# A two-layer transformer chain on one core: Strassen products in all three feed-forward up stages, with half of the weight sums made by adding DMAs

## The chip, the cores and the metric

One core of one Trainium2 chip runs the whole program. The metric is the device time in microseconds of one execution. Three executions were timed; one more was profiled.

## The reference, cut to what matters

The block works on 528 tokens (16 meta tokens and 512 of the sequence) of width 1024. It has forgetting attention, an HGRN2 mixer and a hybrid mixer (retention and stick-breaking attention), each followed by a feed-forward. The change concerns the three feed-forwards. Stages 0 and 1 are the convolutional ones of the first block, stage 2 is the plain one of the second block and works on 512 tokens.

```python
D_FF = ((8 * D_MODEL // 3 + 127) // 128) * 128

def conv_ffn(h, norm_g, w_gate, w_up, conv_w, conv_b, w_down):
    xn = rms_norm(h, norm_g)
    a = xn @ w_gate
    L = a.shape[1]
    a_pad = jnp.pad(a, ((0, 0), (CONV_WIDTH - 1, 0), (0, 0)))
    a = (conv_b + conv_w[0] * a_pad[:, 0:L] + conv_w[1] * a_pad[:, 1:L + 1]
         + conv_w[2] * a_pad[:, 2:L + 2])
    return (jax.nn.silu(a) * (xn @ w_up)) @ w_down
```

All inputs are float32, and the result has to keep about that precision.

## The kernel before

**Layout.** Activations are kept with features on the partitions: `h` is 128 x 8 x 528 (`KT` = 8 feature tiles, `L` = 528 tokens, `META` = 16, `FT` = 22 hidden tiles). A float32 product is made of three passes on TensorE. Every operand is split into a rounded high part and a remainder (`xh`, `xl` for activations, `wh`, `wl` for weights), and the passes are `wh*xh`, `wh*xl` and `wl*xh`. ScalarE rounds a weight unit into `wh` (`act_hi`, L448), VectorE makes the remainder `wl` (`dve_lo`, L452). SyncE (SP) loads weight units of 8 x 128 x 128 (512 KB) into the four slots of `raw`; `wh` and `wl` have two slots each. A slot of `raw` is loaded again once the unit in it has been split.

**Phases.** A `Phase` is a run of n iterations of groups. A group (`pe_group`, L460 to L494) is one output tile of 128 features: 8 k tiles, three passes, and two halves of 264 columns (L489), or one matmul of 512 columns for a "narrow" group (L485). Its sum lies in a pair of PSUM banks, which VectorE reads. Each engine has its own program; what orders the work is the order in which each engine's instructions are written, and the semaphores between them (`mm_done`, `psum_free`, `w_hi`, `w_split`, `w_loaded0` to `3`, `x_ready`, `hid_ready`).

**The up stages 0 and 1** (`PH_UP0`, `PH_UP1`; `up` on ScalarE from L1378 and on VectorE from L2084) have 11 iterations of four groups: gate tile, up tile, gate tile, up tile. VectorE scales the gate by `rstd` out of PSUM into `pre`, ScalarE and VectorE do the three taps of the convolution (L1391, L2101, L2104), ScalarE the silu, VectorE scales the up tile and multiplies (L2111), and the hidden tile is split into `hidh` (L1327) and `hidl` (L2118) at once. In stage 1 the up groups are narrow. The down stage follows, 8 groups of 22 k tiles, and VectorE adds each to the residual (`residual`, `dve_add_h`), makes `xh` and `xl` for the next stage, and goes on.

**The up stage 2** already uses a Strassen scheme (Winograd's form) for 18 of its 22 hidden tiles: after `PH_UP2` (2 iterations of classic groups) comes `PH_DUO2`. A "pair" there is one gate tile and one up tile. The 8 k tiles are cut into two fours, the 512 tokens into two halves of 256 columns (`h1`, `h2`), so gate and up together are a 2 x 2 by 2 x 2 block product. It takes 7 half products of 4 k tiles x 3 passes (84 matmuls of 256 columns, L1281) in place of 8. The sums of the x halves (`xa`, `xb`, `xc`, `xd`) are made once, by VectorE and ScalarE, during the classic iterations. The four sums of the weights of a pair are made by VectorE (`w_sum`, L2810). The seven weight pieces use four half slots of `wh` and `wl`, so a piece is rounded (ScalarE) and its remainder made (VectorE, `duo_lo`, L2814) only when the piece that had its slot before has been multiplied. The results of the products are combined by ScalarE, which copies two out of PSUM (`p_one` and the first half of `pre`), and VectorE, which makes five combinations from PSUM (L2851, L2855, L2864, L2877, L2828) and scales by `rstd` (L2880). Each hidden tile is kept in float32 (`hid2`), since the x sums lie where the rounded hidden tiles go; most of the splits of the hidden tiles are made at the end of the stage and early in the down stage.

**GpSimd (POOL)** sums squares for the norms, loads tables, and does little else; its DMAs in the attention (`crep`, L1963) are its largest use. In the up stages it has no work.

The functions that the change touches:

Of the kernel before, what the change touches and what calls it, by code (L numbers as in the profile page):

```python
# [15 lines left out]
F32 = mybir.dt.float32  # L16
# [3 lines left out]
ALU = mybir.AluOpType  # L20
# [56 lines left out]

class Phase:
# [26 lines left out]
FOX_STEPS, HG_STEPS = 3 * (FOX_H // 2), 3 * HG_H  # L105
# [9 lines left out]
PH_UP1 = Phase(PH_HGOUT, FT // 2, K8, narrow=(1, 3))  # L115
PH_DOWN1 = Phase(PH_UP1, 2, [list(DOWN_K)] * 4, narrow=range(4))
# [15 lines left out]
PH_UP2 = Phase(PH_OUT, 2, K8, [(1, 3, 2 * (_g % 2), 2 - 2 * (_g % 2))[(b - _g) % 4] for b in range(4)], narrow=range(4))  # L132
PH_DUO2 = Phase(PH_UP2, FT // 2 - PH_UP2.n, K8)
PH_DOWN2 = Phase(PH_DUO2, 2, [list(DOWN_K)] * 4, narrow=range(4))

DUO_SLOT, DUO_BANK = (0, 1, 2, 3, 0, 1, 2), (4, 5, 6, 7, 4, 6, 7)
DUO_RANK, DUO_RANK0 = (2, 3, 4, 1, 5, 6, 7), (1, 2, 3, 4, 5, 6, 7)
DUO_FREE = (-2, -1, 0, -3, 1, 2, 3)  # L140
DUO_PAIRS = 2 * PH_DUO2.n
DUO_W = SEQ // 2
# [43 lines left out]
def program(nc, ctx, dram, out):  # L186
# [118 lines left out]
    hid2 = place("hid2", [P, FT, L], F32, arena + 4 * FT * L)[0]  # L305
    a = Area(arena + 3 * 4 * L, arena + 4 * FT * L)

    def x_sum(name):
        at = a.at
        hi, lo = (a.take(f"{name}{part}", [P, KT // 2, DUO_W], F32R) for part in ("h", "l"))  # L310
        return hi, lo, place(f"{name}f", [P, KT // 2, DUO_W], F32, at + 4 * KT // 2 * DUO_W)[0]

    xb, xc, xa = x_sum("xb"), x_sum("xc"), x_sum("xa")
    w_sum1, w_sum2 = (a.take(n, [P, KT // 2, P]) for n in ("w_sum1", "w_sum2"))
    xd = x_sum("xd")
    x_tmp = place("x_tmp", [P, KT // 2, DUO_W], F32, norms_at + 4 * 5 * L)[0]
    p_one, p_two, p_three = sq[:, 0, 0:DUO_W], sq[:, 0, DUO_W:2 * DUO_W], sq[:, 1, 0:DUO_W]
    h1, h2 = slice(META, META + DUO_W), slice(META + DUO_W, L)
# [198 lines left out]
    def dve_x(dve, rx, m, gain_row, t0=0):  # L517
        dve.wait_ge(s("xh_ready"), KT * rx + 1 + m)
        nc.vector.scalar_tensor_tensor(row(xl, m)[:, t0:L], row(h, m)[:, t0:L], col(gains, m + gain_row),  # L519
                                       row(xh, m)[:, t0:L].bitcast(F32), ALU.mult, ALU.subtract).then_inc(s("x_ready"), 1)  # L520
# [2444 lines left out]
```

## Time and profile before

| | us |
|---|---|
| median of 3 runs | 2821.1 (2818.9 to 2822.27) |
| profiled execution, time | 2822.06 |
| profiled execution, span | 2820.4 |
| granted TensorE clock, mean | 0.993 of full |
| TensorE matmuls busy | 2751.6 (98%) |
| VectorE busy | 1702.2 (60%) |
| ScalarE busy | 1252.3 (44%) |
| GpSimd busy | 186.0 (7%) |

Times in the profile are microseconds unless marked ns. PE is TensorE, PEld its weight loads, DVE VectorE, ACT ScalarE, POOL GpSimd, SP SyncE; an engine's name with a q is its queue or sequencer. Matmuls are pipelined, so one that lasts 285 ns may start 122 ns after the one before; the distance of the starts is what counts. A row of a timeline gives start, duration, engine, line, operation, output and inputs, how many instructions are merged in it, and in brackets the idle time before it and what ended that.

### The profile page before, as it was taken

To read this page: it belongs to the slowest core of one execution; us is meant where nothing else is said; L and a number is where in the kernel's file an instruction comes from. 1 tells how busy PE (TensorE), PEld (TensorE's weight loads), DVE (VectorE), ACT (ScalarE), POOL (GpSimd) and SP (SyncE) were. 2 spreads that over 40 slices of the span, in tenths; PEclk is the share of its full clock that TensorE was granted. 3 is DMA by queue.
4 is the path that set the end of the run, shared out by engine and by line. 5 is a ranking of instruction groups with operands and counts; after the bars stand their busy time and mean duration, and the time that the engine had idled before them with its cause. 6 is when DMAs were issued, how large, how long until landed. Compare 5 with 4: busy or idle time off the path is not lost.

```text
span 2820.4 us, 48705 instructions
## 1 busy us (share of the span) xinstructions
PE 2751.6 (98%) x18309; PEld 2492.4 (88%) x18309; DVE 1702.2 (60%) x2639; ACT 1252.3 (44%) x2071; POOL 186.0 (7%) x160
## 2 busy tenths in 40 slices
PE   7999999999989999999999999999999999899998
PEld 7899899999989999899988887888799988689986
DVE  6777745554367776655543453644577776589932
ACT  4445543332245555433322232232478884455632
POOL 2000010000021221000001010010100000100000
PEclk9999999999999999999999999999999999999999
DMA  4222123332331111233333322323222112223332
GB/s 124 68 75 67 53 81 92 89 89 83 94 98 53 53 55 49 68 97 89 97 89 98 94 68 85 92 70 97 72 71 60 58 58 85 76 83 104 103 90 76
DMA packets 417679, 225.74 MB, mean 80 GB/s; under 512 B 7493, under 2 KB 414278, under 8 KB 417462
## 3 DMA queue, kind: packets, MB, share of 16 engines
q1 hardware_dynamic: 414550, 211.45, 26.2%
q0 software_dynamic: 2256, 10.32, 1.2%
q10 hardware_dynamic: 784, 2.75, 0.3%
q8 instruction: 60, 0.98, 0.1%
q14 instruction: 29, 0.24, 0.0%
HBM read 222.36 MB, written 2.13 MB: 80 GB/s over the span
## 4 chain that ended last, share of the span: by engine, by line
PE 56%; DVE 4%; issue 2%; ACT 1%; POOL 0%; DVEq 0%; POOLq 0%; ACTq 0%
PE ps L485 27%; PE ps L489 14%; PE ps L1281 6%; PE ps L1122 2%; PE ps L1163 1%; PE ps L1152 1%; PE ps L1184 1%; PE ps L964 1%; PE ps L1089 1%; DVE wl L452 1%; PE ps L1075 0%; DVE rl L2554 0%; PE ps L1156 0%; PE ps L1110 0%; PE ps L1103 0%
## 5 line engine op out<-in xcount | busy, mean ns | idle before, releaser
L448 ACT ACTIVATE wh<-raw 128x1024 fp32r<-128x1024 f32 (+3 forms) x386 | 385.7, 1001 | 604.8 <-PE ps L489 335.1
L452 DVE TENSOR_TENSOR wl<-raw,wh 128x1024 fp32r<-128x1024 f32 (+3 forms) x386 | 461.8, 1196 | 316.7 <-ACT wh L448 313.7
L489 PE MATMUL ps<-xh,wh 128*128 128x264 f32 x2736 | 569.8, 289 | 9.8 <-DVE xl L519 5.8
L489 PE MATMUL ps<-xl,wh 128*128 128x264 f32 x2736 | 558.4, 285 | 0.0
L489 PE MATMUL ps<-xh,wl 128*128 128x264 f32 x2736 | 558.3, 286 | 0.0
L489 PEld LDWEIGHTS ps<-xh,wh 128*128 128x128 f32 x2736 | 428.8, 189 | 19.6 <-issue 8.8
L489 PEld LDWEIGHTS ps<-xl,wh 128*128 128x128 f32 x2736 | 425.9, 189 | 0.0
L489 PEld LDWEIGHTS ps<-xh,wl 128*128 128x128 f32 x2736 | 425.2, 189 | 0.0
L485 PE MATMUL ps<-xh,wh 128*128 128x512 f32 x672 | 269.4, 401 | 3.5 <-DVE wl L452 3.5
L485 PE MATMUL ps<-xl,wh 128*128 128x512 f32 x672 | 265.7, 395 | 0.0
L485 PE MATMUL ps<-xh,wl 128*128 128x512 f32 x672 | 264.3, 393 | 0.0
L485 PEld LDWEIGHTS ps<-xh,wh 128*128 128x128 f32 x672 | 126.2, 188 | 34.6 <-issue 6.1
L485 PEld LDWEIGHTS ps<-xh,wl 128*128 128x128 f32 x672 | 126.4, 188 | 28.6
L485 PEld LDWEIGHTS ps<-xl,wh 128*128 128x128 f32 x672 | 126.1, 188 | 28.3 <-issue 1.4
L485 PE MATMUL ps<-hidh,wh 128*128 128x512 f32 x352 | 139.6, 396 | 3.9 <-issue 3.5
L485 PE MATMUL ps<-hidh,wl 128*128 128x512 f32 x352 | 139.5, 396 | 0.0
L485 PE MATMUL ps<-hidl,wh 128*128 128x512 f32 x352 | 138.7, 394 | 0.0
L2063 DVE TENSOR_TENSOR rt<-ps,rstd 128x512 f32<-128x512 f32 (+1 forms) x53 | 37.0, 698 | 140.2 <-PE ps L485 100.7
L2063 DVE TENSOR_TENSOR pre<-ps,rstd 128x528 f32<-128x528 f32 (+1 forms) x48 | 33.9, 706 | 121.8 <-PE ps L489 110.4
L532 POOL COPY ssq<-sq 128x528 f32<-128x528 f32 (+1 forms) x6 | 4.6, 760 | 1345.8 <-ACT sq L515 1075.7
L1978 POOL TENSOR_TENSOR g_d<-post_t 128x528 f32<-128x528 f32 (+1 forms) x56 | 68.5, 1241 | 246.6 <-ACT g_e L1533 158.4
L485 PEld LDWEIGHTS ps<-hidh,wh 128*128 128x128 f32 x352 | 66.5, 189 | 19.2 <-issue 3.7
(444 smaller groups left out, 5177.9 us busy)
## 6 DMA issues: line engine op xcount, KB each, us to landing
raw<-in_w_in SPq DMA_DIRECT2D x88, 512.0 KB, 4.1
raw<-in_ffn_w_gate SPq DMA_DIRECT2D x44, 512.0 KB, 3.8
raw<-in_ffn_w_up SPq DMA_DIRECT2D x44, 512.0 KB, 3.8
raw<-in_w_ffn_in SPq DMA_DIRECT2D x44, 512.0 KB, 4.1
raw<-in_fox_w_in SPq DMA_DIRECT2D x33, 512.0 KB, 4.1
raw<-in_hgrn_w_in SPq DMA_DIRECT2D x32, 512.0 KB, 4.1
raw<-in_ffn_w_down SPq DMA_DIRECT2D x32, 448.0 KB, 3.6
raw<-in_ffn_w_down SPq DMA_DIRECT2D x16, 512.0 KB, 3.8
```

The costliest lines, as they stand in the source:

```text
L448: nc.scalar.activation(wh[:, v % 2, 0:nk, :], raw[:, v % RAW_SLOTS, 0:nk, :], ACT.Copy).then_inc(s("w_hi"), 1)
L452: nc.vector.tensor_tensor(wl[:, v % 2, 0:nk, :], raw[:, v % RAW_SLOTS, 0:nk, :], wh[:, v % 2, 0:nk, :].bitcast(F32), ALU.subtract).then_in ...
L485: last = nc.tensor.matmul(ps[:, bank, 0:SEQ], w[:, slot, kk, :], x[:, k0 + k, x.shape[2] - SEQ:x.shape[2]], start=first, stop=end_)
L489: last = nc.tensor.matmul(ps[:, bank + b, 0:HALF], w[:, slot, kk, :], x[:, k0 + k, b * HALF:(b + 1) * HALF], start=first, stop=end_)
L964: last = nc.tensor.matmul(ps[:, 2 + k % 2, P * c:P * (c + 1)], left[:, P * c:P * (c + 1)], right[:, P * c:P * (c + 1)], start=True, stop=True)
L1089: last = nc.tensor.matmul(flat[0:TOK[j], at:at + SEQ - QFIRST[j]], rt[:, 2 + c, P * j:P * j + TOK[j]], rt[:, c, META + QFIRST[j]:L], start ...
L1122: last = nc.tensor.matmul(ps[:, 4 + e, QFIRST[j]:SEQ], r_vt[0:k, j, P * e:P * (e + 1)], r_s[0:k, QSTRIP[j]:QSTRIP[j] + SEQ - QFIRST[j]], s ...
L1152: nc.tensor.matmul(flat[:, QSTRIP[j]:QSTRIP[j] + SEQ - QFIRST[j]], s_kp[:, b, P * j:P * j + P], q[:, QFIRST[j]:SEQ], start=(j < 3 and n == ...
L1163: return nc.tensor.matmul(dst, w[:, :], src, start=False, stop=last, skip_group_check=True)
L1281: last = nc.tensor.matmul(ps[:, DUO_BANK[p], 0:DUO_W], duo_slot(w, p)[:, k, :], x[:, k, :], start=(p < 4 and k + n == 0), stop=(k == KT // ...
L1978: nc.gpsimd.tensor_tensor(hgrn_halves(g_d[:, hgrn_buffer(n), 0:cols_], n), b, b[:, :, width - 1:width].to_broadcast([P, cols_ // (2 * widt ...
L2063: return V.tensor_tensor(shown(ph, gj, dst), out_of(ph, gj), shown(ph, gj, rstd[:, :]), ALU.mult)\
```

## The change

1. The pairs of stage 2 become a general scheme that all three up stages use (`DUO_STAGES` = 0, 1, 2). Each has 2 classic iterations (4 hidden tiles), then 9 iterations of two pairs. The columns of a half are 264 in stage 0, 258 in stage 1 (tokens 12 to 528) and 256 in stage 2.
2. The order of the seven products is new. A pair's product 5 runs ahead of the last product of the pair before. Results are partial sums in PSUM: two banks of `duo_bank(mm)` and bank `y`. After product 5, ScalarE copies the partial sum from one bank to the bank beside it (`fork`), and products go on adding on both sides with `start=False`. Two short matmuls with `start=True` at the beginning of a stage clear the forked banks first. ScalarE makes three copies out of PSUM in a pair (the fork, `p_two`, `p_three`), VectorE two combinations of half width, and scales both halves of the gate in one instruction.
3. Two of the four weight sums of a pair are made by DMAs (`ADDED_STAGES` = 0, 1, 2): POOL issues a copy of 256 KB of gate weights into a buffer, an adding DMA of 256 KB of up weights onto it, and an adding DMA of 256 KB of up weights onto half of the raw slot. VectorE makes the other two.
4. In stages 0 and 1 the hidden tiles, too, are kept in float32 (`hid`) without the factor `rstd` of the up tile, and rounded and split late. The down stage therefore multiplies each result by `rstd` ahead of the residual addition.
5. The x sums are made for each stage, on both engines, between the classic groups.
6. At the end of the pairs ScalarE and VectorE split the first down weights in two halves ahead of the last product.

The diff, cut to its core:

```diff
+DUO_STAGES, ADDED_STAGES = (0,1,2), (0,1,2)
+DUO_FIRST = 2
+DUO_PAIRS = FT - 2 * DUO_FIRST
...
-PH_UP0 = Phase(PH_FOXOUT, FT // 2, K8)
-PH_DOWN0 = Phase(PH_UP0, 2, [list(DOWN_K)] * 4)
+PH_UP0 = Phase(PH_FOXOUT, DUO_FIRST if 0 in DUO_STAGES else FT // 2, K8)
+PH_DUO0 = Phase(PH_UP0, FT // 2 - PH_UP0.n, K8)
+PH_DOWN0 = Phase(PH_DUO0, 2, [list(DOWN_K)] * 4)
...
+DUO_START, DUO_W = (0, META - 4, META), (L // 2, (SEQ + 4) // 2, SEQ // 2)
```

On TensorE, a product and a pair:

```diff
+            def product(i, mm, j, bank, begin=False, last=False):
+                pe.wait_ge(s("p_split"), duo_split(n, i, mm, j, last))
+                hi, lo = x_parts[j][0:2]
+                for k in range(KT // 2):
+                    for nn, (wt, x) in enumerate(((wh, hi), (wh, lo), (wl, hi))):
+                        done = nc.tensor.matmul(ps[:, bank, 0:w], duo_slot(n, wt, j)[:, k, :], x[:, k, :],
+                                                start=begin and k + nn == 0, stop=k == KT // 2 - 1 and nn == 2,
+                                                skip_group_check=True)
+                done.then_inc(s("p_mm"), 1)
+
+            def pair_(i, mm, last=False):
+                g, begin, bank, y = 2 * i + mm, duo_begins(i, mm), duo_bank(mm), duo_bank_y(n)
+                pe.wait_ge(s("p_copied"), copied + 3 * g + 1)
+                if begin:
+                    pe.wait_ge(s("x_ready"), x_before(rx) + KT + DUO_XS)
+                product(i, mm, 0, bank + 1)
+                product(i, mm, 1, bank)
+                pe.wait_ge(s("p_copied"), copied + 3 * g + 2)
+                product(i, mm, 2, bank + 1)
...
+                product(i, mm, 3, y, True)
+                pe.wait_ge(s("p_copied"), copied + 3 * g + 3)
+                product(i, mm, 4, bank + 1)
+                if not last:
+                    if not begin:
+                        pe.wait_ge(s("p_out"), outs + 3 * g - 1)
+                    j, mn = duo_next(i, mm)
+                    product(j, mn, 5, duo_bank(mn), True)
+                pe.wait_ge(s("p_out"), outs + 3 * g + 1)
+                product(i, mm, 6, y, False, last)
...
+            pe.wait_ge(s("p_split"), duo_split(n, 0, 0, 5))
+            for mm in range(2):
+                nc.tensor.matmul(ps[:, duo_bank(mm) + 1, 0:w], duo_slot(n, wh, 5)[:, 0, :], xh[:, 0, h1], start=True, stop=True)
+            product(0, 0, 5, duo_bank(0), True)
```

On ScalarE, the fork:

```diff
+            def fork(i, mm):
...
+                b = duo_bank(mm)
+                copy(ps[:, b + 1, 0:w], ps[:, b, 0:w]).then_inc(s("p_copied"), 1)
```

On GpSimd, the DMAs of a pair:

```diff
+            def pair_(i, mm):
+                g = 2 * i + mm
+                slot, count = duo_unit(n, i, mm, 1)
+                if not first(i):
+                    pool.wait_ge(s("p_split"), duo_split(n, i - 1, mm, 3))
+                pool.dma_start(w_sum[mm][:, :, :], f[0](i, P * mm)[:, 0:4, :]).then_inc(s("pool_dma"), 16)
+                pool.wait_ge(s("pool_loaded0"), added_base(n) + 16 * g)
+                pool.wait_ge(s("pool_dma"), added_base(n) - 16 * (FOX_H // 2) + 16 * g + 32)
+                carry(pool, "pool_carry")
+                pool.dma_start(w_sum[mm][:, :, :], f[1](i, P * mm)[:, 0:4, :], accum_op=ALU.add)\
+                    .then_inc(s("pool_loaded0"), 16)
+                pool.wait_ge(s(f"w_loaded{slot}"), 16 * count)
+                pool.wait_ge(s("pool_loaded1"), added_base(n) + 16 * g)
+                carry(pool, "pool_carry")
+                pool.dma_start(raw[:, slot, 0:4, :], f[1](i, P * mm)[:, 4:8, :], accum_op=ALU.add)\
+                    .then_inc(s("pool_loaded1"), 16)
```

On VectorE, one pair:

```diff
+                if not begin:
+                    before = duo_before(i, mm)
+                    late_half(*before)
+                weight_sum(i, mm, 3)
+                lo(i, mm, 2)
+                if not begin:
+                    if n < 2:
+                        conv_rest(g + 3, 1 - mm)
+                    else:
+                        product(*before)
+                lo(i, mm, 4)
+                if not begin and n < 2:
+                    product(*before)
...
+                    lo(j, mn, 5)
+                lo(i, mm, 6, last)
...
+                V.tensor_tensor(t2[:, h2], ps[:, y, 0:w], p_three, ALU.subtract).then_inc(s("p_out"), 1)
...
+                    weight_sum(j, mn, 1)
+                    if not added:
+                        weight_sum(j, mn, 2)
+                    lo(j, mn, 0)
+                dve.wait_ge(s("p_mm"), duo_mm(n, i, mm, 4))
+                V.tensor_tensor(pre[:, mm, 2 + DUO_START[n]:L + 2].rearrange("p (g t) -> p g t", g=2), ps[:, b:b + 2, 0:w],
+                                rstd[:, DUO_START[n]:L].rearrange("p (g t) -> p g t", g=2), ALU.mult).then_inc(s("p_out"), 1)
+                if not last:
+                    lo(j, mn, 3)
+                    lo(j, mn, 1)
```

On VectorE, in down stages 0 and 1:

```diff
+                    if skip:
+                        dve.wait_ge(s("mm_done"), group_end(ph, i, mm))
+                        hm, tmp = (shown(ph, mm, t) for t in (row(h, 4 * i + mm), post_t[:, mm % 2, :]))
+                        V.tensor_tensor(tmp, out_of(ph, mm), shown(ph, mm, rstd[:, :]), ALU.mult).then_inc(s("dve_step"), 1)
+                        dve.wait_ge(s("dve_step"), steps + 4 * i + mm + 1)
+                        V.tensor_tensor(hm, hm, tmp, ALU.add).then_inc(s("psum_free"), 1)
```

The `w_sum` buffers of the first kind lie in the scratch of the norms, one for each of two pairs in turn. SP loads a pair's gate slot after the fifth piece of the pair two back has been split, and its up slot after the last.

## Rows read from the trace of the kernel before

**Rows 1.** The page, busy us (share of the span) xinstructions.

```profile
PE 2751.6 (98%) x18309; PEld 2492.4 (88%) x18309; DVE 1702.2 (60%) x2639; ACT 1252.3 (44%) x2071; POOL 186.0 (7%) x160
```

**Rows 2.** Busy time by stretch: span, PE, PEld, DVE, ACT, POOL, PEclk, DMA share, GB/s.

```profile
410.00:660.00 250.00, 250.00 (x2042) 249.87 (x2042) 139.61 (x171) 92.00 (x110) 0.00 (x0) 1.00 0.31 90
1190.00:1420.00 230.00, 230.00 (x1451) 208.66 (x1450) 132.36 (x164) 85.18 (x104) 0.00 (x0) 1.00 0.32 92
2495.00:2665.00 170.00, 169.26 (x1423) 168.43 (x1424) 164.51 (x306) 92.24 (x168) 0.00 (x0) 1.00 0.36 99
```

**Rows 3.** Timeline of PE, first matmuls of stage 0 and of the down stage.

```profile
403.98 0.41 PE L489 MATMUL ps<-xh,wh 128*128 128x264 f32 x2
...
663.29 0.40 PE L489 MATMUL ps<-hidh,wh 128*128 128x264 f32 x2
```

**Rows 4.** Timeline of PE, stage 1, first matmuls of two gate tiles in succession.

```profile
1307.37 0.40 PE L489 MATMUL ps<-xh,wh 128*128 128x264 f32 x2
...
1318.77 0.40 PE L489 MATMUL ps<-xh,wh 128*128 128x264 f32 x2
```

**Rows 5.** Timeline of PE, stage 2, two pairs' first matmuls, and two between.

```profile
2554.28 0.28 PE L1281 MATMUL ps<-xh,wh 128*128 128x256 f32 x1
...
2555.94 0.28 PE L1281 MATMUL ps<-xbl,wh 128*128 128x256 f32 x1
...
2559.95 0.28 PE L1281 MATMUL ps<-xah,wl 128*128 128x256 f32 x1
...
2564.32 0.28 PE L1281 MATMUL ps<-xh,wh 128*128 128x256 f32 x1
```

**Rows 6.** Timeline of DVE, stage 2, from one pair's L2864 to the next's.

```profile
2560.81 0.42 DVE L2864 TENSOR_TENSOR t<-ps,sq 128x256 f32<-128x256 f32 x1
...
2564.98 0.69 DVE L2814 TENSOR_TENSOR wl<-w_sum,wh 128x512 fp32r<-128x512 f32 x1
...
2566.18 0.42 DVE L2828 TENSOR_TENSOR t<-ps,sq 128x256 f32<-128x256 f32 x1
2566.51 0.68 DVE L2810 TENSOR_TENSOR w_sum<-w_sum,raw 128x512 f32<-128x512 f32 x1
...
2570.79 0.42 DVE L2864 TENSOR_TENSOR t<-ps,sq 128x256 f32<-128x256 f32 x1
```

**Rows 7.** Timeline of DVE, stage 0, the convolution's two steps.

```profile
415.84 0.76 DVE L2101 SCALAR_TENSOR_TENSOR t<-pre,conv,t 128x528 f32<-128x528 f32 x1
416.75 0.77 DVE L2104 SCALAR_TENSOR_TENSOR t<-pre,conv,t 128x528 f32<-128x528 f32 x1
```

**Rows 8.** Groups of ACT, stage 2: busy us, mean ns, idle before us, releasers.

```profile
L1327 ACT ACTIVATE wh<-raw 128x512 fp32r<-128x512 f32 x64 | 40.3, 629 | 24.4 <-PE ps L1281 24.4
```

**Rows 9.** The page, DMA issues: queue, xcount, KB each, us to landing.

```profile
raw<-in_w_ret_out SPq DMA_DIRECT2D x32, 256.0 KB, 2.8
...
crep<-c_scratch POOLq DMA_DIRECT2D x16, 264.0 KB, 3.5
```

**Rows 10.** Groups of POOL, whole run: its DMA issues in the attention.

```profile
L1963 POOL DMA_DIRECT2D crep<-c_scratch x16 | 8.6, 538 | 260.3 <-DVE t_rows L2212 258.0 <-DMA c_scratch<-fx 2.2
```

**Rows 11.** DMA queues and issues, stage 2, 2500 to 2660 us: packets, MB, share.

```profile
q1 hardware_dynamic: 33280, 16.78, 38.1%
...
raw<-in_w_ffn_in SPq DMA_DIRECT2D x32, 512.0 KB, 4.7
```

**Rows 12.** Waits of PE, 2425 to 2500 us: total, times, longest us.

```profile
PE ps L1281 <- DVE wl L2814: 2.4, 1, 2.4
PE ps L1281 <- DVE xdl L2796: 1.7, 1, 1.7
```

**Rows 13.** Timeline of PE, first matmuls of down stage 2.

```profile
2677.81 0.47 PE L485 MATMUL ps<-hidh,wh 128*128 128x512 f32 x1 [3.49 <-issue]
...
2681.08 0.63 PE L485 MATMUL ps<-hidl,wh 128*128 128x512 f32 x1
...
2681.51 0.63 PE L485 MATMUL ps<-hidh,wl 128*128 128x512 f32 x1
```

More of the change, by code:

```diff
@@ new lines, in duo_source, with duo_begins, duo_next, duo_bank @@
+    def duo_source(n, i, mm, j):
+        gate, up_ = (raw[:, duo_unit(n, i, mm, k)[0], :, :] for k in range(2))
+        w_sum = duo_areas[n][2]
+        return (w_sum[2][:, :, :], gate[:, 4:8, :], up_[:, 0:4, :], w_sum[mm][:, :, :], w_sum[2][:, :, :], gate[:, 0:4, :],
+                up_[:, 4:8, :])[j]
+    def duo_begins(i, mm):
+        return first(i) and mm == 0
+    def duo_next(i, mm):
+        return (i, 1) if mm == 0 else (i + 1, 0)
+    def duo_bank(mm):
+        return 4 + 2 * mm
+    def duo_bank_y(n):
+        return PH_DOWN[n].bank(1) + 1
@@ new lines, in duo_mm, with duo_before, cols @@
+    def duo_mm(n, i, mm, j, last=False):
+        g = 2 * i + mm
+        return duo_base(n, 7) + 7 * g + (7 if last and j == 6 else j + 2)
+    def duo_before(i, mm):
+        return (i, 0) if mm else (i - 1, 1)
+    def cols(w, first, step, k0=0, nk=KT):
+        rows_ = w[P * k0:P * (k0 + nk), :].rearrange("(k p) n -> p k n", p=P)
+        return lambda i, c: rows_[:, :, bass.ds(i * step + (first + c), P)] if not isinstance(i, int) \
+            else rows_[:, :, first + c + i * step:first + c + i * step + P]
@@ L618, in _, with duo_weights @@
+    def duo_weights(n):
+        gate, up_ = ((dram["ffn_w_gate"][n], dram["ffn_w_up"][n]) if n < 2 else
+                     (dram["w_ffn_in_2"][0][:, 0:F], dram["w_ffn_in_2"][0][:, F:2 * F]))
+        return [cols(w, 2 * P * PH_UP[n].n, 2 * P) for w in (gate, up_)]
     @block.sync
@@ L655, in up, with duo, body @@
             stream(ph, lambda i, uj: (fu if uj % 2 else fg)(i, P * (uj // 2)))
+        def duo(n):
+            if n not in DUO_STAGES:
+                return
+            f, base = duo_weights(n), duo_base(n, 7)
+            def body(i):
+                for uj in range(4):
+                    mm, k = divmod(uj, 2)
+                    slot, count = duo_unit(n, i, mm, k)
+                    if first(i):
+                        sp.wait_ge(s("w_split"), unit(PH_DUO[n], 0, uj) + 1)
+                    else:
+                        sp.wait_ge(s("p_split"), base + 7 * (2 * i + mm - 2) + (8 if k else 5))
+                    sp.dma_start(raw[:, slot, :, :], f[k](i, P * mm)).then_inc(s(f"w_loaded{slot}"), 16)
+            body(0)
+            loop(sp, PH_DUO[n].n, body, 1)
         def down(ph, w):
@@ L1919, in duo_body @@
[L1919 to L1927 removed]
+        up(2, PH_UP2, 6)
         for m in range(KT):
```

874 lines of the change are left out of this document (509 added, 365 removed).

## The prediction

> **What bounds the kernel now.** I read the page's busy line first: TensorE's matmuls are busy for 98% of the span, VectorE 60%, ScalarE 44% [rows 1]. The reader is to see that only TensorE is near its limit over the whole run, so the next view is a table by stretch: the first two up stages (from 410 and 1190 us) and the Strassen part of the third (from 2495 us). In the first two TensorE is never idle and VectorE has 56 to 58%; in the third TensorE has 99.6% but VectorE 97% [rows 2]. So in stages 0 and 1 the number of matmuls sets the time, and there the other engines have room. In stage 2 the same change has already been paid for, and VectorE has none. All three run at the full granted clock, 2.4 GHz [rows 2].
>
> The timeline gives the price of a matmul. Stage 0 lasts from 403.98 to 663.29 us [rows 3]: 259.3 us for 22 feature tiles of 96 matmuls (2 projections x 8 k x 3 passes x 2 halves) and about 1.0 us for the norm's sum, so 258.3 / 2112 = 0.1223 us for 264 columns. In stage 1 one feature tile takes 1318.77 - 1307.37 = 11.40 us [rows 4] (48 of 264 columns, 24 of 512). In stage 2 the present Strassen pair takes 2564.32 - 2554.28 = 10.04 us for 84 matmuls of 256 columns; away from its one small gap they follow at (2559.95 - 2555.94) / 34 = 0.1179 us [rows 5], that is 9.91 us a pair.
>
> **Part 1: fewer matmuls in stages 0 and 1.** 4 classic feature tiles stay, 18 become pairs of 7 half products x 4 k x 3 passes = 84 matmuls. Stage 0 keeps 264 columns: 12 matmuls x 0.1223 x 18 = **-26.4 us**. Stage 1 has 258 columns, which no row shows; between 0.1179 at 256 and 0.1223 at 264 a straight line gives 0.1190, so 10.0 us a pair and (11.40 - 10.00) x 18 = **-25.2 us**. At the ends of that bracket it would be 27.0 or 20.3.
>
> **Part 2: stage 2's pairs.** The order changes, the 84 matmuls don't. At best the gap goes: (10.04 - 9.91) x 18 = **-2.3 us**.
>
> **Part 3: what the helpers do in a pair.** VectorE's present pair is 18 instructions, in 2570.79 - 2560.81 = 9.98 us. A 128x512 takes (2566.18 - 2564.98) / 2 = 0.60 us from start to start, a 128x256 from PSUM 0.33 us [rows 6]. The change takes away two of four weight sums and two of five combinations out of PSUM, and merges a third with the scaling of the gate into one read of PSUM. In stage 2 that leaves 11 x 0.60 + 2 x 0.33 = 7.3 us. In stages 0 and 1 the convolution comes on top, two steps of which one waits for the other: 0.91 us from start to start and 0.77 us [rows 7]. That makes 9 x 0.60 (seven remainders, two sums), 1.7, some 0.65 each for product and gate, 2 x 0.34: 9.1 us in a pair of 10.0 to 10.3. It lies beside TensorE, but only with some 10% to spare; were all four sums kept, it would be 10.3 and VectorE would be the bound. ScalarE has seven roundings (0.63 us, and now much idle before them [rows 8]), three copies out of PSUM and two convolution steps, under 7 us. I followed one pair instruction by instruction: with TensorE's products 1.47 us apart each remainder is ready 1.3 us or more before its product. The forked partial sum needs a copy ps to ps on ScalarE ahead of product 0. It is started a product earlier, right after product 5, while product 6 of the pair before runs, and costs TensorE nothing; without that cover it would be the 0.4 us of such a copy in each pair, 22 us, which the second rival holds. The two clearing matmuls of a stage cost 0.25 us.
>
> **Part 4: the adding DMAs.** Each pair gets three transfers of 256 KB on POOL's queue: a copy, an add onto it, an add into the raw slot. No row shows an adding DMA, nor a POOL transfer in runs of 512 bytes. The nearest: a load of 256 KB from SP lands in 2.8 us, one of 264 KB from POOL in 3.5 us [rows 9], and occupies POOL for 0.54 us [rows 10]. POOL has nothing else to do there. The first add waits for the copy to land, the second for the up weights, whose load SP issues after the last remainder of the pair two back (it lands in 4.7 us in this stretch [rows 11]) and so has landed as the previous pair begins. That leaves some 10 us for the second add and 11 us for the first. Latency is thus covered by a factor of two or three. Throughput is tighter: the 1024 KB that a pair loads today take 38.1% of the 16 DMA engines [rows 11]. The 256 KB copy adds 9.5%. If an add costs as much as a copy, the sum is 67%; the cover is gone when one add costs (100 - 38.1 - 9.5) / 2 = 26%, or 2.75 copies. I take the cost as **0**, since the chain and the share both fit at up to twice the row's price; the ends are 0 and the third rival's price.
>
> The Trainium skill (Collectives: The Full Stack, Part 3) says that a reduction in the DMA engines is half as fast as a copy because each piece needs two source reads. By that rule, which no row here tests, the estimate would be 38.1 + 9.5 + 38 = 86%, still under the bound.
>
> **Part 5: beginnings and ends.** Stage 2 now loses 2.4 us as its pairs begin and 1.7 us after the first product, for remainders that VectorE makes late [rows 12]. The new order makes the x remainders earlier. It still has a wait of about 1 us, because the first fork comes after product 5 and the last classic work. At the end of the pairs TensorE idles 3.49 us, and then the clock is lower: matmuls start 0.43 us apart in place of (11.40 - 48 x 0.1223) / 24 = 0.23 [rows 4, 13], for 7 matmuls or so, 1.4 us more. Now the first down weights are rounded ahead of the last product, which should clear most of both. So stage 2: -4.1 - 4.9 + 1.0 + 0.5 = **-7.5 us**. Stages 0 and 1 have no such waits today and get some: 1.0 us at the fork, 0.5 us at the head (16 half-width x sums and ScalarE's rounding of them squeeze between classic weight splits that must be ready every 5.9 us), 0.5 us at the end (16 deferred hidden splits of 0.60 us against 0.73 us of matmuls each), and 0.75 us because the residual now needs a scaling ahead of the addition on the way into the next stage. Together **+5.5 us** in the two. SP's queue has one more kind of wait, with the same loads in the same order.
>
> **Sum**: -26.4 - 25.2 - 2.3 - 7.5 + 5.5 = **-55.9 us**. The profiled execution took 2822.06 us around a span of 2820.4; **2766 us** follows. The median of the three runs, 2821.1, is 1.0 us below that execution; the bounds below are much wider, and I leave it aside.
>
> **Rivals.**
> - *The forecast case* (0.65): own range 2756 to 2779, from the bracket of stage 1 (+5), and from Part 5 (-4 to +7).
> - *VectorE or a hand-over takes part of it back* (0.17). The pair is ordered so tightly that TensorE waits in each pair, as it does now for 0.13 us. For it: 9.1 of 10.0 us in stage 1. Against it: my walk finds slack before each product. At 0.5 us for each of 54 pairs that is 27 us, so 2794 us.
> - *The adding DMAs become the bound* (0.15). Place: the 16 DMA engines and POOL's chain of copy, add, add in each pair; ScalarE's rounding of the two sums is what waits, then TensorE. It decides from 2.75 copies for one add, or from a landing time of 10 us. At 4 copies the share is 38.1 + 9.5 + 76 = 124%, a pair takes 12.4 in place of 10.1 us, and 54 x 2.3 = 124 us make it 2891, slower than before; at 3.3 copies the share is 110% and 54 x 1.0 us give everything back. For it: no row shows such a transfer, all data come in 512-byte packets, 29 ns each by 38.1% x 16 x 160 us / 33280 [rows 11], and an add must fetch its destination as well. Against it: more than half of the engines' time is free.
> - *Beginnings cost more than taken* (0.03): 5 us of idle in each of three stages, followed by the lower clock as in [rows 13], 2785 us or so.
>
> **How the numbers follow.** The time is the first case's. A range of 2756 to 2798 holds it and the second; what is above it is the third. A run of this kernel can be told from no change at about 0.2%, 5.6 us: the first two cases are faster by far more, and so is the last. Of the third, most is slower, a little lands within 0.2%. So faster 0.84, within 0.2% 0.03, slower 0.13.
>
> **What the profile of the changed kernel would show.** Right: by a table by stretch, pairs in stage 0 of 10.3 us, in stage 1 of 10.0, in stage 2 of 9.9; TensorE busy throughout; VectorE near 90% in the first two and 75% in the third; the DMA share between 65 and 90%; adds that land within 8 us; stage 0 lasting 235 us in place of 259. Wrong: roundings of the weight sums that wait for a DMA, a pair longer than 10.5 us, idle of TensorE ended by VectorE once in each pair, a lower granted clock in the pairs.

## The result, and the profile of the changed kernel

Before: 2821.1 us. Changed: **2771.7 us** (median of 4 runs, 2769.2 to 2776.1), a ratio of 0.983 with a 95% interval of 0.981 to 0.984. Two later series of five runs of the same kernel gave 2771.4 and 2771.9. The forecast was 2766 us in a range of 2756 to 2798. The profiled execution is the slowest of the four: 2776.1 us around a span of 2774.4, so it is 46.0 us shorter than the profiled one of before. The steps below are read from these two executions.

The page, busy line (as [rows 1]), and busy time by stretch (as [rows 2]: span, PE, PEld, DVE, ACT, POOL, PEclk, DMA share, GB/s) for the pairs of stages 0, 1 and 2:

```profile
PE 2709.4 (98%) x18315; PEld 2463.5 (89%) x18315; DVE 1801.6 (65%) x2893; ACT 1366.7 (49%) x2401; POOL 363.8 (13%) x322
```

```profile
460.00:620.00 160.00, 160.00 (x1314) 159.91 (x1314) 137.72 (x232) 97.89 (x186) 50.01 (x45) 1.00 0.85 177
1215.00:1375.00 160.00, 159.76 (x1325) 158.76 (x1324) 139.83 (x236) 98.63 (x189) 51.33 (x46) 1.00 0.86 176
2462.00:2622.00 160.00, 159.43 (x1328) 158.50 (x1327) 120.73 (x206) 90.56 (x174) 51.38 (x46) 1.00 0.86 175
```

TensorE has stayed the bound in all three stages, at the full granted clock (1.00, 2.4 GHz), and VectorE has dropped from 97% to 75% in stage 2. The new figure is the last but one: the 16 DMA engines are busy for 85 to 86%, where they were at 31 to 36%.

The timeline of PE: the first matmul of stage 0 and of its down stage (as [rows 3]), then, in stage 1, the first matmul of the product of `xb` (product 0) in three pairs running:

```profile
404.88 0.40 PE L529 MATMUL ps<-xh,wh 128*128 128x264 f32 x2
...
639.80 0.51 PE L529 MATMUL ps<-hidh,wh 128*128 128x264 f32 x2
```

```profile
1298.87 0.28 PE L919 MATMUL ps<-xbh,wh 128*128 128x258 f32 x1
...
1308.91 0.28 PE L919 MATMUL ps<-xbh,wh 128*128 128x258 f32 x1
...
1319.25 0.28 PE L919 MATMUL ps<-xbh,wh 128*128 128x258 f32 x1
```

Stage 0's up stage takes 639.80 - 404.88 = 234.9 us, 24.4 less than before. In stage 1 the first pair shown takes 10.04 us, the next 10.34: a **late pair**. Most pairs of a stage take one and the same time (10.23, 10.04 and 10.02 us in stages 0, 1 and 2), and a few take up to 0.8 us more. Cut into segments at such first matmuls, the two executions differ by:

| segment | before | after | difference | predicted |
|---|---|---|---|---|
| up stage 0 | 259.3 | 234.9 | -24.4 | -26.4 + 2.0 |
| up stage 1 | 253.3 | 233.3 | -20.0 | -25.2 + 2.0 |
| up stage 2, and its down stage | 422.1 | 416.7 | -5.4 | -2.3 - 7.5 |
| down stages 0 and 1 | 249.8 | 250.3 | +0.5 | +1.5 |
| all the rest, unchanged code | 1635.9 | 1639.2 | +3.3 | 0 |

The last line is in part chance. The stretch ahead of stage 1, 388.9 us here, took 386.0 in the second profiled execution of the changed kernel (its span was 2769.2 us), and the mean granted clock over that stretch was 0.98 here and 0.99 there. But 1.6 us of it come back each time: from down stage 1 to stage 2 it was 830.5 us before, 832.1 here and 831.9 to 833.1 in every later profiled execution with the new stages 0 and 1. In the first 30 us of that stretch the granted clock was 1.00 before and is 0.94 now, that is, part of the time TensorE has the lower of its two levels (1.2 GHz). No run was made to show why, and one execution with the old stages 0 and 1 (run 8) also took 831.9.

The end of stage 2 (as [rows 13]), where 3.49 us of idle and a low clock were:

```profile
2633.00 0.28 PE L919 MATMUL ps<-xdh,wl 128*128 128x256 f32 x1
2633.34 0.47 PE L525 MATMUL ps<-hidh,wh 128*128 128x512 f32 x1
2633.65 0.40 PE L525 MATMUL ps<-hidl,wh 128*128 128x512 f32 x1
2633.88 0.39 PE L525 MATMUL ps<-hidh,wl 128*128 128x512 f32 x1
2634.11 0.39 PE L525 MATMUL ps<-hidh,wh 128*128 128x512 f32 x1
```

The down stage follows without idle and its matmuls start 0.23 us apart from the second on.

Where a late pair comes from is seen in the timelines of POOL, ScalarE (ACT) and TensorE around 2550 us:

```profile
2536.41 1.09 POOL L2169 DMA_DIRECT2D w_sum1a<-in_w_ffn_in  x1
2545.26 1.27 POOL L2173 DMA_DIRECT2D w_sum1a<-in_w_ffn_in  x1 [7.75 <-issue]
2546.41 1.43 POOL L2178 DMA_DIRECT2D raw<-in_w_ffn_in  x1
2547.16 1.47 POOL L2169 DMA_DIRECT2D w_sum1b<-in_w_ffn_in  x1
```

```profile
2548.17 0.62 ACT L1439 ACTIVATE wh<-raw 128x512 fp32r<-128x512 f32 x1
2551.68 0.63 ACT L1439 ACTIVATE wh<-w_sum1a 128x512 fp32r<-128x512 f32 x1 [2.89 <-DMA w_sum1a<-in_w_ffn_in]
```

```profile
2553.82 0.39 PE L919 MATMUL ps<-xbh,wh 128*128 128x256 f32 x1 [0.25 <-DVE wl L2425]
```

The copy (L2169) is issued at 2536.41. The add onto it (L2173) follows 8.85 us later, after the copy has landed, and lands in another 6.4 us, just before ScalarE begins the sum's rounding at 2551.68. ScalarE was ready for the sum 2.89 us earlier. TensorE then waits for remainders, a few tenths of a microsecond at a time. In the median pair of stage 2 the add follows its copy after 7.5 us and lands in 4.8, and the sum is there 0.6 us before ScalarE rounds it: the chain of copy and add takes 12.1 us of the time that it has, and next to nothing is left. The queues and the landing times in the same stretch (as [rows 11]):

```profile
q0 software_dynamic: 17535, 12.05, 47.3%
q1 hardware_dynamic: 31614, 15.93, 38.3%
...
raw<-in_w_ffn_in SPq DMA_DIRECT2D x30, 512.0 KB, 5.7
raw<-in_w_ffn_in POOLq DMA_DIRECT2D x16, 256.0 KB, 6.7
w_sum1b<-in_w_ffn_in POOLq DMA_DIRECT2D x16, 256.0 KB, 5.5
w_sum1a<-in_w_ffn_in POOLq DMA_DIRECT2D x14, 256.0 KB, 6.4
```

POOL's three transfers per pair take 47.3% of the engines' time; three copies at 9.5% would be 28.5%. SP's loads land in 5.7 us in place of 4.7. The two lines of `w_sum1` mix copies and adds. By line of the kernel, the copies (L2169), issued about 1 us behind the adding DMA before them, land in 6.9 us, the first adds (L2173) in 4.8 and the second adds (L2178) in 6.7 (medians in this stretch).

### The profile page after: what moved, and what is told of

The parts are those of the page before. It is cut to its first block, busy times and chain, and to the rows that moved or that the text cites. A ratio compares the mean times of both kernels' runs of the same rounds, so it can differ in the third digit from the quotient of the medians.

```text
span 2774.4 us, 50465 instructions
## 1 busy us (share of the span) xinstructions
PE 2709.4 (98%) x18315; PEld 2463.5 (89%) x18315; DVE 1801.6 (65%) x2893; ACT 1366.7 (49%) x2401; POOL 363.8 (13%) x322
## 3 DMA queue, kind: packets, MB, share of 16 engines
q10 hardware_dynamic: 784, 2.75, 0.3%
## 4 chain that ended last, share of the span: by engine, by line
PE 52%; DVE 6%; DMA 5%; issue 4%; ACT 2%; POOL 1%; POOLq 0%; DVEq 0%; ACTq 0%; SPq 0%
PE ps L525 24%; PE ps L529 14%; PE ps L919 4%; PE ps L1110 2%; PE ps L1268 2%; DMA w_sum1a<-in_ffn_w_gate 2%; DMA w_sum1b<-in_ffn_w_gate 1%; PE ps L1309 1%; DMA w_sum1a<-in_w_ffn_in 1%; PE ps L1298 1%; DVE wl L492 1%; PE ps L1330 1%; PE ps L1235 1%; DMA w_sum1b<-in_w_ffn_in 1%; PE ps L1155 1%
## 5 line engine op out<-in xcount | busy, mean ns | idle before, releaser
L529 PE MATMUL ps<-xh,wh 128*128 128x264 f32 x1872 | 394.9, 292 | 11.4 <-DVE xl L559 6.7
L529 PE MATMUL ps<-xl,wh 128*128 128x264 f32 x1872 | 383.1, 286 | 0.0
L529 PE MATMUL ps<-xh,wl 128*128 128x264 f32 x1872 | 382.5, 286 | 0.0
L529 PEld LDWEIGHTS ps<-xh,wh 128*128 128x128 f32 x1872 | 293.6, 190 | 20.8 <-issue 10.7
L529 PEld LDWEIGHTS ps<-xl,wh 128*128 128x128 f32 x1872 | 292.6, 190 | 0.0
L529 PEld LDWEIGHTS ps<-xh,wl 128*128 128x128 f32 x1872 | 291.7, 190 | 0.0
L919 PE MATMUL ps<-xh,wh 128*128 128x264 f32 (+2 forms) x648 | 183.6, 283 | 0.4
L919 PE MATMUL ps<-xh,wl 128*128 128x264 f32 (+2 forms) x648 | 183.2, 283 | 0.0
L919 PE MATMUL ps<-xl,wh 128*128 128x264 f32 (+2 forms) x648 | 183.0, 282 | 0.0
L2425 DVE TENSOR_TENSOR wl<-raw,wh 128x512 fp32r<-128x512 f32 x216 | 145.9, 687 | 28.0 <-ACT wh L1439 28.0
L1439 ACT ACTIVATE wh<-raw 128x512 fp32r<-128x512 f32 x222 | 137.6, 622 | 27.8 <-PE ps L919 16.6
```

The lines of the kernel that those rows point to most:

```text
L529: last = nc.tensor.matmul(ps[:, bank + b, 0:HALF], w[:, slot, kk, :], x[:, k0 + k, b * HALF:(b + 1) * HALF], start=first, stop=end_)
L919: done = nc.tensor.matmul(ps[:, bank, 0:w], duo_slot(n, wt, j)[:, k, :], x[:, k, :], start=begin and k + nn == 0, stop=k == KT // 2 - 1 an ...
L1439: return nc.scalar.activation(dst, src, ACT.Copy, scale=scale)
L2425: V.tensor_tensor(duo_slot(n, wl, j), duo_source(n, i, mm, j), duo_slot(n, wh, j).bitcast(F32), ALU.subtract)\
```

## The experiments

Twelve runs follow, in four groups, each group against runs of before on the same chip (2822.6 to 2823.2 us). A pair is measured from the first matmul of its product of `xb` to that of the next pair. It counts as late from 0.2 us above its stage's median; "excess" is the sum of what pairs took above their stage's median in the profiled execution, without the first and the last pair of each stage. Late pairs and excess come from that one execution, the times from all runs of a series.

**1. The changed kernel again.** No edit.

> The changed kernel once more, as the yardstick for the other kernels of this set. Expected: 2768 to 2776 us, with a few pairs in stages 1 and 2 that take 10.3 to 10.9 us in place of 10.02 to 10.04, at other places than in the first trace if they come from chance in the landing of the DMAs, at the same places if the order of the work makes them.

Measured: 2771.4 us (2770.8 to 2775.4), ratio 0.982 (0.980 to 0.983). Five late pairs, excess 2.9 us, at other places than in the first profiled execution (nine, 4.3 us): stage 1 had none now. Late pairs have no fixed place in the order of work.

**2. The plain copy on SP's queue.** It is issued right behind the gate load, and waits neither for POOL nor for the add before it.

```diff
+ sp.dma_start(duo_areas[n][2][mm][:, :, :], f[0](i, P * mm)[:, 0:4, :]).then_inc(s(f"x_loaded{mm}"), 16)
...
- pool.dma_start(w_sum[mm][:, :, :], f[0](i, P * mm)[:, 0:4, :]).then_inc(s("pool_dma"), 16)
...
- pool.wait_ge(s("pool_dma"), added_base(n) - 16 * (FOX_H // 2) + 16 * g + 32)
+ pool.wait_ge(s(f"x_loaded{mm}"), 16 + 16 * (PH_DUO[n].n * sum(d < n for d in ADDED_STAGES) + i + 1))
```

> The plain copy that begins each weight sum is issued by SP right behind the gate load in place of POOL; POOL keeps the two adding DMAs. Theory A: POOL's chain of copy, landing, add, add takes about a whole pair (10.2 us from one copy's issue to the next in the first trace), so it is the chain that makes some sums late. Then ScalarE's and VectorE's waits for w_sum by DMA vanish, no pair is longer than 10.1 us, and the time is 3 to 6 us below the changed kernel's. Theory B: the 16 DMA engines, 85% busy, make them late. Then the waits stay and the time is the same within 2 us.

Measured: 2770.4 us (2769.4 to 2772.9), 1.0 us less than run 1, ranges overlapping, where theory A had 3 to 6 us. Four late pairs, excess 2.0 us. So taking the copy off POOL's queue does not end them. It helps less than theory A had it, since the copy still lands in 6.2 us: the sum of the median pair of stage 2 is there 1.9 us before ScalarE rounds it, 1.3 us more than in the changed kernel.

**3. Copies in place of adds.** Same DMAs, same sizes, same waits, without the addition; the two sums that DMAs make therefore lack one of their terms.

```diff
- pool.dma_start(w_sum[mm][:, :, :], f[1](i, P * mm)[:, 0:4, :], accum_op=ALU.add)
+ pool.dma_start(w_sum[mm][:, :, :], f[1](i, P * mm)[:, 0:4, :])
...
- pool.dma_start(raw[:, slot, 0:4, :], f[1](i, P * mm)[:, 4:8, :], accum_op=ALU.add)
+ pool.dma_start(raw[:, slot, 0:4, :], f[1](i, P * mm)[:, 4:8, :])
```

> Both adding DMAs become plain copies of the same bytes (the sums lack one of their terms). If an add costs the DMA engines two copies, the DMA share of the pairs falls from 85% to 38 + 3 x 9.5 = 67%, and the sums land 1 to 3 us sooner; if it costs one copy, the share stays at 85%. Theory A on the matmuls of 256 columns, which start 0.1193 us apart here and 0.1179 before: traffic into SBUF slows TensorE's reads, and with less of it they come back part of the way, to 0.1186. Theory B: the new order itself does it (accumulation onto copied sums, one bank shared by both sides), and 0.1193 stays. Time 2 to 5 us below the changed kernel's.

Measured: 2768.0 us (2766.8 to 2769.7), ratio 0.980 (0.979 to 0.982). No late pair at all: the sum of the median pair of stage 2 is there 5.1 us before its rounding, and in no pair less than 2.9. The pairs' common times stay as they were (10.23, 10.04 and 10.02 us). In run 4 stage 2's pairs take 10.02 us too, with 105 GB/s in place of 175. So DMA traffic is not what makes stage 2's matmuls dearer than before: theory A of that text is out. Busy time in stage 2 and the DMA queues there:

```profile
2462.00:2622.00 160.00, 160.00 (x1344) 160.00 (x1343) 122.61 (x210) 93.04 (x178) 32.09 (x43) 1.00 0.61 174
```

```profile
q1 hardware_dynamic: 32145, 16.21, 35.5%
q0 software_dynamic: 3520, 11.54, 25.0%
...
raw<-in_w_ffn_in SPq DMA_DIRECT2D x28, 512.0 KB, 4.7
raw<-in_w_ffn_in POOLq DMA_DIRECT2D x15, 256.0 KB, 3.4
w_sum1a<-in_w_ffn_in POOLq DMA_DIRECT2D x14, 256.0 KB, 4.5
w_sum1b<-in_w_ffn_in POOLq DMA_DIRECT2D x14, 256.0 KB, 4.2
```

The same bytes per second (174 GB/s) take 61% of the engines in place of 86%. So a plain copy costs 25.0 / 3 = 8.3%, an adding one (47.3 - 8.3) / 2 = 19.5%, **2.3 copies**. Run 10, whose POOL queue has adds alone, gives the same without a difference of two runs: 39.9% for 7.87 MB, against 46.1% for the 20.39 MB of SP's copies, 2.2 times as much per byte. In time to landing little of it is the add's own: the first add takes 4.8 us in place of 4.3, while the copy and the second add, which are issued close behind another adding DMA, take 6.9 and 6.7 in place of 4.4 and 3.4. The whole price of adding in place of copying is 3.4 us of the kernel (2771.4 against 2768.0), about the excess of the late pairs.

**4. No adding DMAs.** All four weight sums on VectorE, in all stages.

```diff
-DUO_STAGES, ADDED_STAGES = (0,1,2), (0,1,2)
+DUO_STAGES, ADDED_STAGES = (0, 1, 2), ()
```

> All three stages keep the new order, but VectorE makes all four weight sums and POOL issues nothing. Theory A: VectorE then has 10.3 us of work in each pair of stages 0 and 1 and becomes the bound there: pairs of 10.4 to 10.7 us, TensorE waiting for remainders (wl), 36 x 0.3 = 11 us more in these stages, and 2 to 4 us less in stage 2, where VectorE has room and no DMA is late: 2776 to 2784 us. Theory B: the walk overstates VectorE's work, its instructions overlap more than I allow, and the adding DMAs buy nothing: pairs of 10.24 and 10.04 us, 2766 to 2770 us.

Measured: 2784.3 us (2783.5 to 2785.3), ratio 0.986 (0.985 to 0.988), 13 us above run 1.

```profile
460.00:620.00 160.00, 160.00 (x1271) 156.23 (x1271) 152.26 (x255) 96.54 (x181) 0.00 (x0) 1.00 0.34 99
1215.00:1375.00 160.00, 159.99 (x1280) 155.46 (x1279) 152.11 (x257) 96.09 (x181) 0.00 (x0) 1.00 0.34 99
2462.00:2622.00 160.00, 160.00 (x1344) 160.00 (x1343) 139.57 (x239) 91.59 (x175) 0.00 (x0) 1.00 0.36 105
```

In stages 0 and 1 VectorE is busy for 95%, and TensorE's matmuls fall from 1314 and 1325 to 1271 and 1280 in 160 us. Stage 0 goes from the first product of an x sum to the down stage in 644.0 - 454.2 = 189.8 us for 18 pairs, 10.5 us each, within theory A's 10.4 to 10.7. TensorE still shows as 100% busy there; only the count of matmuls tells that it is held up. In stage 2, without the convolution, VectorE has 87% and pairs stay at 10.02. So the DMAs are worth their place in stages 0 and 1 and next to nothing in stage 2.

**5. The x sums moved by 64 bytes** in stages 1 and 2. This is for another miss: stage 2's pairs take 10.02 us in the changed kernel in every execution, while 84 matmuls at [rows 5]'s 0.1179 make 9.91.

```diff
-            at = arena + 4 * L * (6 + 4 * k)
+            at = arena + 4 * L * (6 + 4 * k) + (64 if n else 0)
```

> The x sums of stages 1 and 2 lie 64 bytes further on in SBUF; nothing else changes. In the kernel before they began at odd multiples of 64 bytes, in the changed one at multiples of 128. Theory A: the place of the moving operand sets the 0.1200 us between two starts that every product on an x sum shows in stage 2, against 0.1176 before. Then these come back to 0.1176, a pair of stage 2 takes 9.92 to 9.95 in place of 10.02 us, one of stage 1 falls by as much or stays, and the time is 1 to 3 us below the changed kernel's. Theory B: the accumulation onto copied sums or the banks do it, and nothing moves.

Measured: 2771.6 us (2768.3 to 2776.2), no gain as a whole. Timeline of PE in stage 2, the 12 matmuls of product `xc` from their first to the first of `xa`; the changed kernel, then the shifted one:

```profile
2475.27 0.28 PE L919 MATMUL ps<-xch,wh 128*128 128x256 f32 x1
...
2476.71 0.28 PE L919 MATMUL ps<-xah,wh 128*128 128x256 f32 x1
```

```profile
2475.73 0.28 PE L919 MATMUL ps<-xch,wh 128*128 128x256 f32 x1
...
2477.14 0.28 PE L919 MATMUL ps<-xah,wh 128*128 128x256 f32 x1
```

1.44 us against 1.41: 0.1200 and 0.1175 us a matmul, from the place of the moving operand alone. (By the kernel's own placement, worked out and not shown in a trace, the sums' rows begin at multiples of 128 bytes in stage 2, and 64 past such a multiple after the edit, as in the kernel before.) Stage 2's common pair falls to 9.91 us as forecast. In stage 1, whose rows are 1032 bytes long, the edit makes pairs longer (10.07 for 10.04). The excess of late pairs was 6.3 us in this execution and took the gain.

**6. Adding DMAs in stages 0 and 1 only.**

```diff
+DUO_STAGES, ADDED_STAGES = (0, 1, 2), (0, 1)
```

> Stage 2 keeps the new order but VectorE makes all its weight sums; the adding DMAs stay in stages 0 and 1. With all sums on VectorE stage 2 had 17 pairs of 10.02 us and none longer, so the late pairs there (0.4 to 2 us in all) should go: 2769 to 2771 us, 0 to 2 us below the changed kernel's. If the adding DMAs were worth something in stage 2, its pairs would be longer than 10.02 us.

Measured: 2770.7 us (2769.9 to 2777.4). Stage 2 has no late pair (excess 1.8 us before), but begins 2.9 us later: from its first matmul to its first product of an x sum 110.7 us pass against 107.8, since VectorE has more sums to make there. In runs 4 and 9, whose stage 2 has no adding DMA either, the same stretch takes 109.3 and 109.1 us: some 1.4 us belong to the sums, the rest to this execution. In the times nothing clear of the scatter is left.

**7, 8. The new order in stage 2 alone**, with and without the adding DMAs.

```diff
+DUO_STAGES, ADDED_STAGES = (2,), (2,)
```

> Stages 0 and 1 are as before (classic groups), stage 2 has the new order and its adding DMAs. By the traces the new stage 2 saves 3.9 us up to the down stage and 1.5 us after it: 2816 to 2819 us. Then stages 0 and 1 account for 44 to 47 us of the change. If the parts of the change helped each other, this would be 2821 or above.

> As the one before, with all weight sums on VectorE. If the new order alone gives stage 2 its room (three copies on ScalarE, two combinations fewer on VectorE), this is as fast or up to 2 us faster: 2814 to 2818 us. If VectorE still needed the help, pairs would be longer than 10.02 us and it would be slower.

Measured: 2817.5 us (2816.8 to 2819.3), ratio 0.998 (0.997 to 0.999), and 2816.4 us (2815.2 to 2820.5), ratio 0.998 (0.997 to 0.999), against 2822.6. Stage 2 thus gives some 5 to 6 us, as the table above has it, and its DMAs add nothing to that. Stages 0 and 1 give the rest, some 46 us.

**9 to 12. Combinations.** In 9 the x sums of stage 2 alone are moved, with adding DMAs in stages 0 and 1:

```diff
+DUO_STAGES, ADDED_STAGES = (0, 1, 2), (0, 1)
...
+            at = arena + 4 * L * (6 + 4 * k) + (64 if n == 2 else 0)
```

> Adding DMAs in stages 0 and 1 only (all four weight sums on VectorE in stage 2), and the x sums of stage 2 alone moved by 64 bytes. Theory A (place of the moving operand, and the share of the DMA engines): stage 2's pairs take 9.91 to 9.95 us with none above 10.1, since VectorE needs about 9.5 us of them without the convolution; the up stage lasts 288 us, stage 1 is as in the changed kernel, and the whole takes about 2768.5 us, 2 us less than with the adding DMAs in stages 0 and 1 alone (2770.7). Theory B (VectorE becomes the bound once a pair is shorter than 10 us): pairs stay at 10.02 us, the remainders of the weights end TensorE's waits, and the time stays at 2770.7.

> The same, and in stages 0 and 1 the plain copy is issued by SP in place of POOL. Theory A: the few late pairs of stages 0 and 1 come from the share of the DMA engines, so they stay, and the time is that of the kernel without this edit, within 1 us. Theory B: POOL's chain (copy, wait, add, add) makes them, so they go and the time falls by 1 to 2 us more.

> The changed kernel once more, beside the two combinations: 2771 to 2772 us by both theories. By theory A the first combination is 2 to 3 us faster in the same rounds, by theory B at most 1 us.

> The kernel x_shift_in_2_copy_on_sp kept the adding DMAs in all three stages (its text on record says stages 0 and 1: that edit was not in it). This is the same kernel with the plain copy left on POOL's queue, so that nothing but the copy's queue differs. Theory A (only the share of the DMA engines makes late pairs): the copy's queue plays no part, 2766 to 2767 us, as with the copy on SP. Theory B (POOL's chain of copy, wait, add, add makes them once the share is high): stage 2 shows three or more pairs above 10.2 us, as in the three looks at the changed kernel, and the time is 2769 to 2770.5 us; the changed kernel's 2771.9 less 1.9 us for 18 shorter pairs.

Run 9 came as theory A had it: pairs of stage 2 take 9.91 us, none is late, and 2768.7 us (forecast 2768.5) are 2.0 below run 6 of the series before, which differs by the place of the x sums alone. Theory B, pairs that stay at 10.02 us, is out.

Run 10 was not what its text says: the line with the stages was left as in the changed kernel, so it has the adding DMAs in all three stages, the plain copy on SP, and the x sums of stage 2 moved. Run 12 was made to have its exact partner.

| run | adds in | copy issued by | us (lowest to highest) | late pairs | excess |
|---|---|---|---|---|---|
| 9 x_shift_in_2 | 0, 1 | POOL | 2768.7 (2765.6 to 2769.9) | 0 | 0 |
| 10 x_shift_in_2_copy_on_sp | 0, 1, 2 | SP | **2766.4** (2764.7 to 2766.8) | 0 | 0 |
| 11 after_third, no shift | 0, 1, 2 | POOL | 2771.9 (2770.1 to 2773.9) | 4 | 2.5 |
| 12 x_shift_in_2_all_adds | 0, 1, 2 | POOL | 2771.9 (2770.5 to 2774.8) | 7 | 3.9 |

Run 10's ratio is 0.9795 (0.978 to 0.981) against before, 5.5 us under the changed kernel in the same series (run 11) without overlap of the runs. Run 12 stood in another series, on another chip; before took 2822.7 us in both. Stages 1 and 2 of runs 12 and 10, by stretch:

```profile
1215.00:1375.00 160.00, 159.53 (x1328) 158.78 (x1327) 139.84 (x236) 99.23 (x189) 50.58 (x46) 1.00 0.85 176
2462.00:2622.00 160.00, 159.47 (x1349) 158.99 (x1348) 121.86 (x209) 92.41 (x176) 51.42 (x46) 1.00 0.87 177
```

```profile
1215.00:1375.00 160.00, 160.00 (x1341) 160.00 (x1340) 141.53 (x240) 99.31 (x192) 40.00 (x32) 1.00 0.88 176
2462.00:2622.00 160.00, 160.00 (x1358) 160.00 (x1357) 123.67 (x212) 93.58 (x180) 38.52 (x30) 1.00 0.86 177
```

The share of the DMA engines is as high in run 10 as in run 12 (0.88 and 0.86 against 0.85 and 0.87), yet TensorE never waits in these stretches and runs 9 and 13 matmuls more in 160 us. So the share alone is not the cause, and theory A's 2766 to 2767 us for run 12 did not come. Theory B names the right place, POOL's chain, but its numbers did not come either: two late pairs in stage 2 where it had three or more (and five in the other stages), and 2771.9 us where it had 2769 to 2770.5. Nor is the whole 5.5 us the copy's: late pairs are 3.9 us of the 8.0 between the two profiled executions, and 2.8 us lie ahead of stage 0 (406.3 against 403.5 us, at a granted clock of 0.98 against 0.99), in code that no edit touches.

ScalarE's waits for the weight sums, stage 2, 2462 to 2622 us (total, times, longest us), in run 12, then run 2, then run 10:

```profile
ACT wh L1439 <- DMA w_sum1a<-in_w_ffn_in: 5.7, 3, 3.0
ACT wh L1439 <- DMA w_sum1b<-in_w_ffn_in: 3.8, 3, 1.6
```

```profile
ACT wh L1443 <- DMA w_sum1a<-in_w_ffn_in: 3.8, 2, 2.8
```

```profile
ACT wh L1443 <- DMA w_sum1b<-in_w_ffn_in: 3.1, 2, 1.6
```

The longest wait tells a late pair from a harmless one. The ten traces with adding DMAs have 44 late pairs. ScalarE waits 24 times for 2.2 us or more for the sum of copy and add; each time this pair or the next is late or both are, which makes 41. The other three follow waits of 1.5 to 1.6 us, and no shorter wait makes a late pair. So a late pair comes from a sum that lands some 1.5 us or more after ScalarE is ready for it, and what counts is the slack of that chain, 0.6 us in the changed kernel's median pair of stage 2, 1.9 in run 2, 2.0 in run 10, 5.1 in run 3. Run 2's four late pairs come from two sums that landed 2.7 and 2.8 us too late. Why single landings are that late, and whether run 10 had none by more than chance (its five times lie within 2.1 us), stays open; the profiles show one execution of each.

## Why the prediction was right, point by point

It forecast 2766 us and 2771.7 came, inside the range, and the likeliest case is the one that happened. 5.7 us are missing; in the profiled executions it is -55.9 against -46.0: 3.3 us outside the segments, 4.4 in stage 2, 3.2 in stage 1, less 1.0 in the down stages. Two sums of the text are a little off without weight: 2766 + 27 is 2793, not 2794, and the terms named for the forecast case's own range reach down to 2760, not 2756.

- **Part 1, stage 0: right.** -24.4 for the segment, as forecast. A pair takes 10.23 us where 84 x 0.1223 = 10.27 was put.
- **Part 1, stage 1: 3.2 us too much.** The straight line gave 0.1190 us for 258 columns; the rows give 10.04 / 84 = 0.1195, which is 0.7 us over 18 pairs. Late pairs took another 1.9. The rest is within the bounds of Part 5.
- **Part 2, stage 2's pairs: wrong in sign.** -2.3 was forecast, from a pair of 10.04 us; but old pairs of 10.04 and 9.96 us alternate, 10.00 on average. The new ones take 10.02 and on average 10.13 with the late ones, so +2.4. The step said "the order changes, the 84 matmuls don't" and took [rows 5]'s 0.1179 us along; but the x sums also moved in memory, and run 5 shows that this alone makes 0.1200 of 0.1175.
- **Part 3, VectorE: right.** Forecast 9.1 us of 10.0 to 10.3 in stages 0 and 1 and 7.3 in stage 2; the rows show 137.72 / 160 x 10.23 = 8.8, 139.83 / 160 x 10.04 = 8.8 and 120.73 / 160 x 10.02 = 7.6. "Were all four sums kept, it would be 10.3 and VectorE would be the bound": run 4 shows 10.5 us a pair and a kernel 13 us slower.
- **Part 4, the adding DMAs: right that they don't bind, wrong that they cost 0, and wrong on the latency.** In the text's own copies of 9.5% an add costs 19.5 / 9.5 = 2.05 of them, between the one copy and the bound at 2.75 (26%), and the share is 86%. That is the figure which the rule of the Trainium skill (Collectives: The Full Stack, Part 3) gave, half the speed of a copy for two source reads; this trace agrees with it, and by run 3's own copies it is 2.3 for 2. The page's reason, the two source reads, no run here shows. "Latency is thus covered by a factor of two or three" failed. It rested on landings of 2.8 and 3.5 us. The copy lands in 6.9 us and the add follows, so that copy and add take 12.1 us in the median pair, 15.3 in the late pair above, and the cover is 0.6 us, not a factor. The text's own signs of being wrong came with it: roundings of the sums that wait for a DMA (five in stage 2, 9.7 us in all), and single pairs above 10.5 us (up to 10.86). Most of these waits cost nothing, as ScalarE and TensorE had slack behind them, and so the price was 3.4 us (run 3) and the forecast held.
- **Part 5: stage 2 right, the way into the next stages open.** Its segments lost 5.4 us although the pairs gained 2.4, so beginnings and end gave -7.8 against -7.5. The wait for the fork is 0.5 us in each stage, not 1.0. Inside the down stages of 0 and 1 the scaling cost 0.5 us in both together; the term was 1.5, for the way into the next stage. Behind down stage 1 another 1.6 us appear in every profiled execution with the new stages 0 and 1, with the lower granted clock told above. Whether they belong to this term stays open.
- **The rivals.** The hand-over in each pair (0.5 us, 2794 us) did not come: away from late pairs TensorE waits only the 0.5 us at each stage's fork. The DMA bound (2891 us) decides when one add takes 26% of the engines; it takes 19.5%. But its chain of copy, add, add gave a mild form of that case: a tail of late pairs at a share of 85 to 86%.

## What to carry to other kernels

An adding DMA is a way to take an elementwise sum off a full VectorE, and here it was worth 13 us; but count it as 2.3 copies of engine time, and plan its chain on landings as they are beside the other transfers, and on the worst, not the median one: copies that land in 4.4 us when nothing adds took 6.9 here, and up to 8.6. Then follow the chain to the engine that waits for it, and count its slack in microseconds. When a tile of a moving operand gets a new place, its matmuls need not keep their price; read the distance of starts again. And take a mean over a whole stage, not one pair, as the price of before.

## What the runs showed that was not expected

- A matmul with 256 moving columns starts 0.1200 or 0.1175 us after the one before it, depending on the moving operand's place, 64 bytes apart (run 5); over 18 pairs that is 1.9 us. No such difference was expected.
- When two of three transfers add, POOL's queue moves 12.05 MB in 17535 packets; when all three are copies, 11.54 MB in 3520 (3.3 KB each). With adds alone (run 10) it is 7.87 MB in 15840, some 500 bytes each, as in SP's loads. POOL is busy for 1.1 to 1.5 us with the issue of each transfer of the changed kernel, 0.75 when all are copies, not the 0.54 of [rows 10].
- Late pairs come at other places in each execution: nine, five and four in three profiled executions of the same kernel, with an excess of 4.3, 2.9 and 2.5 us.
